# A two-block transformer kernel on one core: some transfers issued by GpSimd, a rotation put ahead of a head's weights, mask additions and first loads moved

## The chip, the cores and the metric

The kernel runs on one core of one Trainium2 chip. The metric is the device time of one execution in microseconds (us), taken as the median of several. "The trace" is the hardware profiler's record of one execution. TensorE is PE in it (PEld its weight loads), VectorE DVE, ScalarE ACT, GpSimd POOL, SyncE SP; a q behind a name is the engine's queue, where DMAs are issued.

## The reference

Two blocks of two layers each work on 256 tokens of width 1024, all in float32.

The first block's layer is a gated feed-forward (width 2816), a mix of pooling over windows of 2 to 16 tokens and causal attention with 8 heads, and a second feed-forward. The second block's layer, which matters here, is cut to its core:

```python
proj = x @ w_in[i]
q_na, k_na, v_na, q_r, k_r, v_r, g_r, gate_a, gate_b = jnp.split(proj, IN_SPLITS, axis=-1)
ya = neighbourhood_attention(q_na, k_na, v_na, na_rpb[i])        # 8 heads of 64
yb = bidirectional_retention(q_r, k_r, v_r, g_r, ...)            # 4 heads; q_r, k_r go through rotary()
merged = sigmoid(gate_a) * (ya @ w_branch_a[i]) + sigmoid(gate_b) * (yb @ w_branch_b[i])
x = layer_norm(ALPHA * x + merged @ w_out[i], ...)
ffn = conv_glu_ffn(x, w_up[i], conv_w[i], conv_b[i], w_down[i])
ple = sigmoid(x @ w_ple_gate[i]) * (p[i] @ w_ple_proj[i])
x = layer_norm(ALPHA * x + ffn + ple, ...)
```

`rotary` takes the halves x1, x2 of a head's 128 features and gives x1 cos - x2 sin and x2 cos + x1 sin. In the neighbourhood attention a query sees the keys of 16 columns around it, with a bias (`na_rpb`) for each offset.

## The kernel before

**Weights.** All weights come as one stream of 336 chunks of 128 partitions x 2048 float32 (1 MB) through three slots. SP loads a chunk as soon as its slot's raw copy is free (L452). ACT writes its upper part (`w_hi`, L614), DVE the rest (`w_lo = raw - w_hi`, L1092), and TensorE makes three products of upper and lower parts for each tile, about 5.7 us for a chunk. A slot's parts may be rewritten when TensorE is done with the chunk (`w_used`), so chunk m is followed in its slot by m + 3. In the code `split_after(here, m)` splits the chunk that follows m.

**Order of work.** Each engine has one program, written out by hand, that runs over the chunks (m = 0 to 41 in the mixing part of a layer of the second block, then 33 chunks of feed-forward as A gate, B up, D down). What an engine does beside a chunk stands in its loop at that m, and is done in that order. Semaphores count events: `mix_evac` the results taken out of PSUM in a layer, `qk_ready` the rotated pairs, `qk_turned` and `v_placed` arrived DMAs (16 each), `prod_ready` the products in a feed-forward.

**Neighbourhood attention, m = 5 to 13.** DVE takes the scores of head m - 5 (`softmax_scores`, L1232 to L1242), ACT their exponentials (L710), DVE scales them (`softmax_weights`, L1249, L1253) and turns the corners of head m - 6 (`turn_corners`, L1272, L1273). TensorE transposes the weights of head m - 6 after chunk m and multiplies two heads with the values (`weigh_near_values`, L2131) after chunks 8, 10, 12 and 14. That needs the corners of both heads and all values in `v_tok`.

**Values and pair halves.** Value rows leave PSUM at m = 5 (`mix_evac` 5 and 6). `place_values` sorts them from row order into `v_tok` by four DMAs for each of two tiles (64 KB each, L746). The retention's q and k are made as pairs n = 0 to 3 of 128 features x 2 x 256 at m = 6 to 9 (`mix_evac` 7 to 10; the first three are sums made by DVE, the last is ACT's evacuation at L964). `turn_halves` (L713) swaps a pair's halves by two DMAs (128 KB each) into one of two places, by n % 2. `turn_pairs` on DVE (L1281, L1282, L1285) multiplies by sine and cosine and adds. Both DMA helpers are issued from ACT's queue here, at m = 5, 6 and 6 to 9, and `turn_pairs(n)` stands at m = n + 7 behind the head's weights and corners, ahead of the split.

**Tables and masks.** `load_tables` on GpSimd (L553) loads `rpb` and `pT` of a layer and adds the window mask to the bias of each head (L561, eight additions). It runs after the pooling for layer 0, and for layer 1 right after the first layer norm of layer 0. GpSimd's `decays` (L579 to L585) come at the head of a layer, and its next work is at the retention.

**First loads.** The first two chunks come in four pieces of 128 x 512 (L437, L439), and the input `xT` in four as well (L782). TensorE runs 22 warm-up matmuls meanwhile (L2140).

## Time and profile before

| | us |
|---|---|
| runs | 1938.16, 1938.36, 1939.33 |
| median | 1938.36 |
| the profiled execution, device time | 1938.22 |
| its span, first to last instruction | 1936.4 |
| TensorE busy in it | 1918.9 (99%) |
| VectorE, ScalarE, GpSimd busy | 1386.9, 1030.9, 167.3 |

The span is what the views below count from: a row of the timeline gives start and duration in us, engine, line, operation, output and inputs, and in brackets the idle time of the engine before it with what ended it. The execution's own time is 1.82 us more than its span. TensorE is the engine that sets the end, so a stretch is read from its gaps.

### The profile page before, as it was taken

To read this page: it belongs to the slowest core of one execution; us is meant where nothing else is said; L and a number is where in the kernel's file an instruction comes from. 1 tells how busy PE (TensorE), PEld (TensorE's weight loads), DVE (VectorE), ACT (ScalarE), POOL (GpSimd) and SP (SyncE) were. 2 spreads that over 40 slices of the span, in tenths; PEclk is the share of its full clock that TensorE was granted. 3 is DMA by queue.
4 is the path that set the end of the run, shared out by engine and by line. 5 is a ranking of instruction groups with operands and counts; after the bars stand their busy time and mean duration, and the time that the engine had idled before them with its cause. 6 is when DMAs were issued, how large, how long until landed. Compare 5 with 4: busy or idle time off the path is not lost.

```text
span 1936.4 us, 26395 instructions
## 1 busy us (share of the span) xinstructions
PE 1918.9 (99%) x9942; PEld 1626.9 (84%) x9942; DVE 1386.9 (72%) x1700; ACT 1030.9 (53%) x1195; POOL 167.3 (9%) x147
## 2 busy tenths in 40 slices
PE   9999999999999999999999999999999999999998
PEld 8888878888888888788888878878888878888887
DVE  7666777666776667768667666577889676677887
ACT  6444665544454455655444554456566554456664
POOL 1000230000000004103002201020001401000000
PEclk9999999999999999999999999999999999999999
DMA  8555545555455545446555554565553654555552
GB/s 335 190 182 185 203 143 185 186 185 192 174 197 194 192 155 209 162 173 228 194 184 186 180 180 152 213 225 182 195 195 138 211 185 160 210 202 192 193 193 111
DMA packets 54362, 365.37 MB, mean 189 GB/s; under 512 B 6416, under 2 KB 7696, under 8 KB 11280
## 3 DMA queue, kind: packets, MB, share of 16 engines
q1 hardware_dynamic: 49392, 349.66, 50.1%
q0 software_dynamic: 1616, 9.96, 1.4%
q10 hardware_dynamic: 3280, 4.72, 0.8%
q8 instruction: 51, 0.84, 0.2%
q14 instruction: 23, 0.19, 0.0%
HBM read 360.12 MB, written 1.05 MB: 187 GB/s over the span
## 4 chain that ended last, share of the span: by engine, by line
PE 92%; DVE 3%; ACT 2%; issue 2%; ACTq 0%; DMA 0%; POOL 0%; POOLq 0%; SPq 0%; DVEq 0%
PE up_two L1865 13%; PE gate_two L1865 13%; PE up_two L1870 7%; PE gate_two L1870 7%; PE gate_two L1796 6%; PE gate_two L1798 5%; PE gate_two L1797 5%; PE low_two L1796 5%; PE low_two L1797 5%; PE low_two L1798 5%; PE bank L1796 5%; PE bank L1798 5%; PE bank L1797 5%; DVE w_lo L1092 1%; PE low_two L1865 1%
## 5 line engine op out<-in xcount | busy, mean ns | idle before, releaser
L1092 DVE TENSOR_TENSOR w_lo<-raw,w_hi 128x2048 fp32r<-128x2048 f32 x315 | 728.7, 2314 | 204.6 <-ACT w_hi L614 198.9
L614 ACT ACTIVATE w_hi<-raw 128x2048 fp32r<-128x2048 f32 x319 | 608.7, 1909 | 102.5 <-PE low_two L1798 32.1
L1865 PE MATMUL up_two<-br_parts,w_hi 128*128 128x512 f32 x1152 | 276.6, 391 | 0.0
L1865 PE MATMUL gate_two<-br_parts,w_hi 128*128 128x512 f32 x1120 | 273.9, 390 | 0.9 <-DVE w_lo L1295 0.7
L1865 PEld LDWEIGHTS gate_two<-br_parts,w_hi 128*128 128x128 f32 x1120 | 209.4, 188 | 45.0 <-issue 1.8
L1865 PEld LDWEIGHTS up_two<-br_parts,w_hi 128*128 128x128 f32 x1152 | 211.9, 188 | 41.4
L1796 PE MATMUL gate_two<-w_lo,br_parts 128*128 128x512 f32 x480 | 192.1, 400 | 1.0 <-ACT area L931 0.9
L1798 PE MATMUL gate_two<-w_hi,br_parts 128*128 128x512 f32 x480 | 187.4, 390 | 0.0
L1797 PE MATMUL gate_two<-w_hi,br_parts 128*128 128x512 f32 x480 | 187.0, 390 | 0.0
L1870 PE MATMUL gate_two<-br_parts,w_lo 128*128 128x256 f32 x1120 | 155.2, 283 | 0.0
L1870 PEld LDWEIGHTS up_two<-br_parts,w_lo 128*128 128x128 f32 x1152 | 148.7, 191 | 5.5
L1870 PE MATMUL up_two<-br_parts,w_lo 128*128 128x256 f32 x1152 | 151.9, 283 | 0.0
L1870 PEld LDWEIGHTS gate_two<-br_parts,w_lo 128*128 128x128 f32 x1120 | 147.2, 191 | 4.9
L669 ACT ACTIVATE hid_hi<-area 128x512 fp32r<-128x512 f32 x58 | 36.7, 632 | 170.5 <-PE bank L1798 107.8
L664 ACT ACTIVATE area<-gate_two 128x512 f32<-128x512 f32 x68 | 40.5, 595 | 136.0 <-PE gate_two L1870 136.0
L664 ACT ACTIVATE area<-up_two 128x512 f32<-128x512 f32 x68 | 40.7, 598 | 130.0 <-PE up_two L1870 129.9
L1796 PEld LDWEIGHTS gate_two<-w_lo,br_parts 128*128 128x128 f32 x480 | 90.1, 188 | 23.1 <-issue 5.7
L1798 PEld LDWEIGHTS gate_two<-w_hi,br_parts 128*128 128x128 f32 x480 | 90.1, 188 | 19.5
L1797 PEld LDWEIGHTS gate_two<-w_hi,br_parts 128*128 128x128 f32 x480 | 90.3, 188 | 17.6
L1149 DVE TENSOR_TENSOR area<-area,up_two 128x512 f32<-128x512 f32 x68 | 46.5, 684 | 62.2 <-ACT area L664 62.2
L1796 PE MATMUL low_two<-w_lo,hid_hi 128*128 128x512 f32 x232 | 91.0, 392 | 0.0
L1797 PE MATMUL low_two<-w_hi,hid_lo 128*128 128x512 f32 x232 | 91.0, 392 | 0.0
(329 smaller groups left out, 2974.4 us busy)
## 6 DMA issues: line engine op xcount, KB each, us to landing
raw<-stream SPq DMA_DIRECT2D x328, 1024.0 KB, 4.8
area<-rows POOLq DMA_DIRECT2D x4, 1024.0 KB, 5.1
area<-rpb POOLq DMA_DIRECT2D x2, 1280.0 KB, 7.6
raw<-stream SPq DMA_DIRECT2D x8, 256.0 KB, 7.5
konst<-consts SPq DMA_DIRECT2D x1, 1600.0 KB, 8.3
area<-rows POOLq DMA_DIRECT2D x2, 768.0 KB, 4.8
area<-xT ACTq DMA_DIRECT2D x4, 256.0 KB, 6.7
x<-x_rows SPq DMA_DIRECT2D x1, 1024.0 KB, 10.9
```

The costliest lines, as they stand in the source:

```text
L614: act.activation(w_hi[:, s, :], raw[:, s, :], ACT.Copy).then_inc(hi_ready[s], 1)
L664: return act.activation(out, pair[:, :, 1, :], ACT.Copy)
L669: act.activation(place[:, 0:2, :], hidden, ACT.Copy).then_inc(hid_hi_ready.sem, 1)
L1092: dve.tensor_tensor(w_lo[:, s, :], raw[:, s, :], w_hi[:, s, :].bitcast(F32), ALU.subtract).then_inc(lo_ready[s], 1)
L1149: return dve.tensor_tensor(out, out, pair[:, :, 0, :], ALU.add)
L1796: pe.matmul(out, whi, xlo, start=start, stop=False, skip_group_check=True)
L1797: pe.matmul(out, wlo, xhi, start=False, stop=False, skip_group_check=True)
L1798: return pe.matmul(out, whi, xhi, start=False, stop=stop, skip_group_check=True)
L1865: pe.matmul(pair[:, f, :, :], w_hi[:, s, at:at + P], parts[:, :, k, :], start=k == 0, stop=False, skip_group_check=True)
L1870: return pe.matmul(pair[:, f, 0, :], w_lo[:, s, at:at + P], parts[:, 0, k, :], start=False, stop=k == DT - 1, skip_group_check=True)
```

## The change

In `place_values` and `turn_halves` the engine becomes GpSimd; they are called in its program between the decays and the retention, values first. `turn_halves` waits for other counts there. `turn_pairs` moves ahead of `softmax_weights` in DVE's loop. `load_tables` waits for a product of a feed-forward: for layer 0 the first of the last one in the first block, for layer 1 the first of layer 0's. The host lays out the first two chunks and `xT` so that each piece is contiguous in HBM, and `stretch` reads them so; what arrives in SBUF is the same.

```diff
@@ -253,6 +253,10 @@
         def piece(j):
             return slice(j * CHUNK // HALVES, (j + 1) * CHUNK // HALVES)
 
+        def stretch(chunk, j):
+
+            return chunk.rearrange("p n -> (p n)").rearrange("(j p n) -> j p n", j=HALVES, p=P)[j]
+
         def by_piece(last, s, pieces):
 
             return [pieces] * (HALVES - 1) + [last[s]]
@@ -434,9 +438,9 @@
 
             sp.dma_start(col1[:, :, :].rearrange("p l c -> p (l c)"), cols1).then_inc(col1_in, 16)
             for j in range(HALVES):
-                sp.dma_start(raw[:, 0, piece(j)], stream[0][:, piece(j)]).then_inc((piece_full[0] + [raw_full[0]])[j], 16)
+                sp.dma_start(raw[:, 0, piece(j)], stretch(stream[0], j)).then_inc((piece_full[0] + [raw_full[0]])[j], 16)
             for j in range(HALVES):
-                sp.dma_start(raw[:, 1, piece(j)], stream[1][:, piece(j)]).then_inc((piece_full[1] + [raw_full[1]])[j], 16)
+                sp.dma_start(raw[:, 1, piece(j)], stretch(stream[1], j)).then_inc((piece_full[1] + [raw_full[1]])[j], 16)
             sp.dma_start(raw[:, 2, :], stream[2]).then_inc(raw_full[2], 16)
             sp.dma_start(konst[:, 0:MATRICES], consts[:, 0:MATRICES]).then_inc(matrices_in, 16)
             for s in range(SLOTS):
@@ -489,6 +493,24 @@
                 for a in range(TT):
                     pool.wait_ge(ln_var.sem, here.at(ln_var, TT * n + a + 1))
                     pool.tensor_tensor(rs[:, a:a + 1], ms[:, a:a + 1], minus_half, ALU.pow).then_inc(ln_rs.sem, 1)
+
+            def place_values(here, tile):
+
+                pool.wait_ge(mix_evac.sem, here.at(mix_evac, 5 + tile))
+                for r in (2 * tile, 2 * tile + 1):
+                    for a in range(TT):
+                        first = r % TT * GRID_W + a * HALF_W
+                        pool.dma_start(v_tok[r:P:GRID_ROWS, a, :], v_by_row[first:first + HALF_W, tile, :]
+                                       ).then_inc(v_placed.sem, 16)
+
+            def turn_halves(here, n):
+
+                two, place = ret_qk[:, 2 * n:2 * n + 2, :], turned_places[n % 2]
+                pool.wait_ge(mix_evac.sem, here.at(mix_evac, n + 7 if n < 2 else 10))
+                if n >= 2:
+                    pool.wait_ge(qk_ready.sem, here.at(qk_ready, n - 1))
+                for at, other in ((0, TURN), (TURN, 0)):
+                    pool.dma_start(place[at:at + TURN], two[other:other + TURN]).then_inc(qk_turned[n % 2].sem, 16)
 
             def load_rows(n):
 
@@ -550,8 +572,9 @@
                                        ).then_inc(pool_d.sem, 1)
                 norm(here, 2)
 
-            def load_tables(l, n):
-
+            def load_tables(l, n, before):
+
+                pool.wait_ge(prod_ready.sem, before)
                 pool.dma_start(area4[:, 0:HEADS * TT * NEAR], rpb[bass.ds(l, 1)].rearrange("a p n -> (a p) n")
                                ).then_inc(bias_in, 16)
                 pool.dma_start(flat(ple_in[:, :, :]), pT[bass.ds(l, 1)].rearrange("a p n -> (a p) n")
@@ -563,7 +586,7 @@
 
 
             pool.wait_ge(pool_y.sem, DEPTH)
-            load_tables(0, 1)
+            load_tables(0, 1, Place(0, DEPTH - 1).at(prod_ready, PAIRS + 1))
             for layer in range(DEPTH):
                 here = Place(1, layer)
                 cur = col2[:, layer, :]
@@ -584,6 +607,12 @@
                 for h in range(RET_HEADS):
                     pool.tensor_tensor(decays[:, h, :], decays[:, h, :], backward[:, h, :], ALU.add
                                        ).then_inc(dist_ready.sem, 1)
+
+                for tile in range(TT):
+                    place_values(here, tile)
+                pool.wait_ge(dist_ready.sem, here.at(dist_ready, RET_HEADS))
+                for n in range(4):
+                    turn_halves(here, n)
 
                 for h in range(RET_HEADS):
                     pool.wait_ge(ret_var.sem, here.at(ret_var, h + 1))
@@ -599,7 +628,7 @@
                 pool.wait_ge(ple_split.sem, here.at(ple_split, 1))
                 layer_norm(here, 0)
                 if layer < DEPTH - 1:
-                    load_tables(layer + 1, layer + 2)
+                    load_tables(layer + 1, layer + 2, here.at(prod_ready, 1))
                 else:
                     pool.wait_ge(base_ready.sem, here.at(base_ready, DT))
                     load_rows(2 * layer + 1)
@@ -711,14 +740,6 @@
                                        accum_out=stat[:, b, 4 + a:5 + a])
                 e.then_inc(exp_ready.sem, 1)
 
-            def turn_halves(here, n, two):
...
             def weights_out(here, h, keys):
 
                 act.wait_ge(p_turned.sem, here.at(p_turned, h + 1))
@@ -737,15 +758,6 @@
                 act.activation(out, banks[6][:, 0, :].rearrange("p (a n) -> p a n", a=TT), ACT.Copy
                                ).then_inc(pT_ready.sem, 1)
 
-            def place_values(here, tile):
...
             def attention_out(here, j):
 
                 act.wait_ge(pv_done.sem, here.at(pv_done, 2 * j + 2))
@@ -779,7 +791,7 @@
                                ).then_inc(by_piece(hi_ready, s, piece_hi[s])[j], 1)
 
             for j in range(HALVES):
-                act.dma_start(flat(x_first[:, 2 * j:2 * j + 2, :]), xT[:, j * 2 * T:(j + 1) * 2 * T]).then_inc(x_in[j], 16)
+                act.dma_start(flat(x_first[:, 2 * j:2 * j + 2, :]), stretch(xT, j)).then_inc(x_in[j], 16)
             act.wait_ge(small_set, SMALL)
             act.activation(ms[:, :], small[:, 0:TT], ACT.Silu)
             act.wait_ge(col1_in, 16)
@@ -941,8 +953,6 @@
                             act.wait_ge(branch_evac.sem, here.at(branch_evac, 2))
                         act.wait_ge(wide_half.sem, here.at(wide_half, wide_ends.index(m) + 1))
                         wide_out(0, m)
-                        if m == 5:
-                            place_values(here, 0)
                     chunk_done(here, m)
                     bank = banks[4 + m % 2]
                     if m in wide_ends:
@@ -978,13 +988,6 @@
                         near_attention_out(here, (m - 8) // 2)
                     if 0 <= m - 5 < HEADS:
                         softmax_exp(here, m - 5, NEAR_KEYS, lambda a: 1.0)
-                    if m == 6:
-                        place_values(here, 1)
-                    if 6 <= m < 10:
-                        if m == 6:
-                            act.wait_ge(dist_ready.sem, here.at(dist_ready, RET_HEADS))
-                        act.wait_ge(mix_evac.sem, here.at(mix_evac, m + 1))
-                        turn_halves(here, m - 6, two)
                     if 0 <= m - 18 < RET_HEADS:
                         h = m - 18
                         act.wait_ge(ret_turned.sem, here.at(ret_turned, h + 1))
@@ -1650,12 +1653,12 @@
                                               ALU.mult).then_inc(ple_mul.sem, 1)
                     if m >= 8 and m % 2 == 0 and (m - 8) // 2 < HALVES:
                         near_attention_lower(here, (m - 8) // 2)
+                    if 7 <= m < 11:
+                        turn_pairs(here, m - 7, ret_qk[:, 2 * (m - 7):2 * (m - 6), :], K_COS2, K_SIN2)
                     if 0 <= m - 5 < HEADS:
                         softmax_weights(here, m - 5, NEAR_KEYS)
                     if 0 <= m - 6 < HEADS:
                         turn_corners(here, m - 6)
-                    if 7 <= m < 11:
-                        turn_pairs(here, m - 7, ret_qk[:, 2 * (m - 7):2 * (m - 6), :], K_COS2, K_SIN2)
                     s = m % SLOTS
                     if m == 33:
                         dve.wait_ge(hi_ready[s], here.uses(m) + 2)
@@ -2464,6 +2467,10 @@
     return part.reshape(-1, P, part.shape[1]).transpose(1, 0, 2).reshape(P, -1)
 
 
+def _stretches(chunk):
+    return chunk.reshape(P, HALVES, -1).transpose(1, 0, 2).reshape(P, -1)
+
+
 def _ffn_chunks(up, down, held=0):
     whole = slice(None)
 
@@ -2519,7 +2526,7 @@
         chunks += _ffn_chunks(a["w_up_2"][l], a["w_down_2"][l], held=1)
     out = np.empty((STREAM, P, CHUNK), np.float32)
     for n, c in enumerate(chunks):
-        out[n] = c
+        out[n] = _stretches(c) if n < 2 else c
     assert len(chunks) == STREAM
     return out
 
@@ -2549,7 +2556,7 @@
     entry = (rows_off + NA_ROWS - 1) * (2 * NA_COLS - 1) + cols_off + NA_COLS - 1
     rpb = a["na_rpb_2"].reshape(DEPTH, HEADS, -1)[:, :, entry].transpose(0, 2, 1, 3, 4).reshape(DEPTH, P, -1)
     arrays = {
-        "xT": _tile(a["x"][0].T, slice(None), slice(None)),
+        "xT": _stretches(_tile(a["x"][0].T, slice(None), slice(None))),
         "x_rows": a["x"][0].reshape(TT, P, D).transpose(1, 0, 2).reshape(P, -1),
         "stream": _stream(a),
         "cols1": cols1,
```

## Rows read from the trace of the kernel before

**Rows 1.** The page's first part, and the cores with span and granted clock.

```profile
PE 1918.9 (99%) x9942; PEld 1626.9 (84%) x9942; DVE 1386.9 (72%) x1700; ACT 1030.9 (53%) x1195; POOL 167.3 (9%) x147
...
core 0: 1936.4 us, clock 0.999
```

**Rows 2.** Start of the kernel: timeline of TensorE, and two windows with DMA share and GB/s.

```profile
1.11 6.98 PE L2140 MATMUL low_two<-softT 128*128 128x256 f32 x22 [1.11 <-POOL small L466]
...
8.40 0.47 PE L1865 MATMUL gate_two<-br_parts,w_hi 128*128 128x512 f32 x1 [0.32 <-DVE w_lo L1295]
...
10.46 0.47 PE L1865 MATMUL gate_two<-br_parts,w_hi 128*128 128x512 f32 x1 [0.43 <-DVE w_lo L1295]
...
2.00:3.00 1.00, 1.00 (x4) 0.73 (x4) 0.00 (x0) 0.35 (x1) 0.00 (x0) 1.00 0.86 197
...
7.00:8.00 1.00, 1.00 (x6) 0.61 (x4) 0.43 (x1) 1.00 (x3) 0.00 (x0) 1.00 1.01 367
```

**Rows 3.** Timeline of TensorE, neighbourhood attention of layer 0: its four gaps.

```profile
1101.96 0.76 PE L2131 MATMUL up_two<-softT,area 128*64 128x160 f32 x8 [0.17 <-issue]
...
1116.35 0.76 PE L2131 MATMUL up_two<-softT,area 128*64 128x160 f32 x8 [0.83 <-issue]
...
1124.67 0.47 PE L1796 MATMUL gate_two<-w_lo,br_parts 128*128 128x512 f32 x1 [0.44 <-ACT area L931]
...
1130.75 0.76 PE L2131 MATMUL up_two<-softT,area 128*64 128x160 f32 x8 [0.36 <-issue]
```

**Rows 4.** Timelines of GpSimd, DVE and TensorE at the first layer norm, layers 0 and 1.

```profile
1275.29 0.57 POOL L555 DMA_DIRECT2D area<-rpb  x1
...
1281.17 9.95 POOL L561 TENSOR_TENSOR area<-area,konst 128x320 f32<-128x320 f32 x8 [4.77 <-DMA area<-rpb]
...
1286.23 4.16 DVE L1107 TENSOR_TENSOR br_parts<-area,br_parts 128x256 fp32r<-128x256 f32 x4
...
1728.01 1.47 DVE L1107 TENSOR_TENSOR br_parts<-area,br_parts 128x256 fp32r<-128x256 f32 x4
...
1286.36 0.50 PE L1808 MATMUL gate_two<-w_lo,br_parts 128*128 128x512 f32 x1 [0.39 <-DVE w_lo L1092]
...
1293.33 0.50 PE L1796 MATMUL low_two<-w_lo,br_parts 128*128 128x512 f32 x1 [1.13 <-DVE w_lo L1092]
```

**Rows 5.** Timelines of ACT (and its queue), DVE and TensorE in the same attention.

```profile
1092.84 1.86 ACTq L720 DMA_DIRECT2D area<-area  x2
1094.75 1.91 ACT L614 ACTIVATE w_hi<-raw 128x2048 fp32r<-128x2048 f32 x1 [3.25 <-issue]
...
1103.29 0.69 DVE L1285 TENSOR_TENSOR area<-area 128x512 f32<-128x512 f32 x1
...
1115.08 0.17 DVE L1249 RECIPROCAL stat<-stat 128x2 f32<-128x2 f32 x1 [1.00 <-ACT soft L710]
...
1108.57 0.28 PE L1798 MATMUL gate_two<-br_parts,w_hi 128*128 128x256 f32 x1
```

**Rows 6.** One line's answer, L720 on ACT's queue; then L523, 256 KB from GpSimd.

```profile
DMA to landing us min/median/max: 3.2/4.5/5.6
...
L523 POOL DMA_DIRECT2D area<-rows x2: 543/547/551, 227.0 to 746.6; - x2
...
DMA to landing us min/median/max: 5.4/5.6/5.7
```

**Rows 7.** DMA issues by line (KB each, median us to landing): pair 2, and the page's tables.

```profile
area<-area ACTq DMA_DIRECT2D x2, 128.0 KB, 4.5
...
area<-rpb POOLq DMA_DIRECT2D x2, 1280.0 KB, 7.6
```

**Rows 8.** Timelines in feed-forwards: DVE and TensorE in layer 0's, GpSimd at 887.

```profile
1337.59 2.29 DVE L1092 TENSOR_TENSOR w_lo<-raw,w_hi 128x2048 fp32r<-128x2048 f32 x1 [1.04 <-ACT w_hi L614]
...
1343.16 0.40 PE L1796 MATMUL low_two<-w_lo,hid_hi 128*128 128x512 f32 x1
...
887.24 13.54 POOL L561 TENSOR_TENSOR area<-area,konst 128x320 f32<-128x320 f32 x8 [8.37 <-DMA area<-rpb]
```

More of the change, by code:

```diff
@@ L712, in softmax_exp @@
                 e.then_inc(exp_ready.sem, 1)
-            def turn_halves(here, n, two):
-                place = turned_places[n % 2]
-                if n >= 2:
-                    act.wait_ge(qk_ready.sem, here.at(qk_ready, n - 1))
-                for at, other in ((0, TURN), (TURN, 0)):
-                    act.dma_start(place[at:at + TURN], two[other:other + TURN]).then_inc(qk_turned[n % 2].sem, 16)
             def weights_out(here, h, keys):
@@ L738, in near_weights_out @@
                                ).then_inc(pT_ready.sem, 1)
-            def place_values(here, tile):
-                act.wait_ge(mix_evac.sem, here.at(mix_evac, 5 + tile))
-                for r in (2 * tile, 2 * tile + 1):
-                    for a in range(TT):
-                        first = r % TT * GRID_W + a * HALF_W
-                        act.dma_start(v_tok[r:P:GRID_ROWS, a, :], v_by_row[first:first + HALF_W, tile, :]
-                                      ).then_inc(v_placed.sem, 16)
             def attention_out(here, j):
```

## The prediction

> **What bounds the kernel now.** I read the profile's page first: TensorE is busy 1918.9 of 1936.4 us and the granted clock is 0.999 [rows 1]. So a change that removes no matmul can win only out of TensorE's 17.5 us without one, and I listed its gaps from the timeline. Those of 0.1 us or more add up to 10.3 us. They are the first 1.11 us, 0.32 and 0.43 us at the first weight pieces [rows 2], four gaps in the neighbourhood attention of each layer of the second block, 0.17 + 0.83 + 0.44 + 0.36 = 1.80 us in its layer 0 and 1.85 us in layer 1 [rows 3], 0.39 + 1.13 = 1.52 us after the first layer norm of layer 0 [rows 4], and 2.4 us at a layer's end that the change doesn't touch. Everything below moves one of these or opens a new one. A measurement of this kernel can tell 0.2%, 3.9 us, from no change.
>
> **Part 1, values and pair halves issued by GpSimd.** Per layer ACT loses 16 DMA issues. Two for a pair's halves take 1.86 us on its queue, and with the four for the values ahead of them they hold the split of chunk 6 back: 3.25 us of idle, until 1094.75 [rows 5]. DVE's low part of that chunk then ends at 1098.9 and DVE trails TensorE by some 4 us for the next five chunks; its period there is 7.2 us (scores at 1106.11 and 1113.31). That lag makes the 0.83 and the 0.36: DVE has the corners of head 3 at 1116.24, after its wait until 1115.08 [rows 5], and TensorE goes on at 1116.35 [rows 3]. With the issues on GpSimd, idle from 1075 until 1160 in this layer, the split starts at 1091.5 and DVE is ahead by 3.2 us minus 0.6 that TensorE's scores cost it, so about 2.6.
>
> GpSimd's queue in order: four value DMAs after the first evacuation (1080.7), four after the second (1083.8), at 0.55 us each [rows 6] done by 1086.1; then pair 0 after its sum (1090.9), pair 1 after 1097.6. These have more than 4 us before DVE wants them. The next one doesn't. Pair 2 used to leave as soon as its sum was made, at 1107.5. Now it waits for count 10 of the evacuations, which ACT's evacuation of chunk 9 gives (count 9 could come from ACT as well as from DVE, and GpSimd, unlike ACT, can't know which). TensorE ends chunk 9 at 1108.7 [rows 5] and ACT needs 0.6 us, so count 10 comes at 1109.35, the two issues are at 1109.4 and 1110.0, and what arrives is the question. Ends for issue to landing: 3.2 us (the fastest of the eight issued by ACT [rows 6]) and 7.6 us (GpSimd's table of 1280 KB [rows 7], far larger). I take 4.6, nearest to the same transfer into the same place, 4.5 from ACT [rows 7]. Arrival: 1114.6.
>
> **Part 2, rotation ahead of the weights.** Per chunk DVE waits 1.00 us for ACT's exponentials (0.41 to 0.67 where a sum fills it) [rows 5], and the rotation (three operations, 1101.89 to 1103.98, 2.1 us) can hide that: 0.4 to 1.0 us of DVE time per chunk, against weights that come 1.1 to 1.7 us later after the scores. By hand for layer 0: at chunk 7 rotation 0 runs 1097.6 to 1099.7, corners done 1100.9, TensorE asks at 1101.8, so the 0.17 goes. At chunk 8 corners are done at 1108.2, in time. At chunk 9 DVE has its scores at 1111.3 but the rotation now stands in front of weights, corners and split, and waits for the arrival at 1114.6; it ends at 1116.7, weights 1117.5, corners 1117.9. TensorE, which asks at 1115.35, goes on at 1118.0: a gap of 2.6 us for 0.83. At chunk 10 DVE has scores 1120.95, lower half 1121.35, rotation 3 (long arrived) 1123.45, weights 1124.15; TensorE asks at 1124.65, no gap. ACT's split no longer stands before its evacuation of chunk 11, so the 0.44 goes: chunk 12 starts at 1125.8 for 1124.67, +1.1. The 0.36 goes too (corners 1129.9, asked 1131.5). **+0.8 us a layer, +1.6 for both.** Each 1 us of landing moves this by 1 us: at 3.2 us it is -0.6, with the old gaps at -1.8 the floor; at 5.6 (slowest of the eight) +1.8; at 7.6 +3.8.
>
> The rows price the issue (0.55 us [rows 6]) but not this transfer from GpSimd; its nearest in size, 256 KB, landed in 5.6 us behind one of 768 KB [rows 6]. The Trainium skill (DMA: Bandwidth & Descriptors, Latency and other measured facts) gives a first byte after about 1 us for a transfer issued by GpSimd and 0.6 for one by ACT; by that the landing would be 0.4 us more, the sum 0.8 more. No row has the same transfer from both.
>
> **Part 3, masks in the next feed-forward.** In layer 0 the eight additions of the window run at 1281.17 for 9.95 us, right in the layer norm. DVE's four subtractions of a tile pass take 4.16 us there and 1.47 in layer 1, which loads no tables [rows 4]. With the other operations in that stretch DVE loses some 4.6 us, and 0.39 + 1.13 us of it reach TensorE; layer 1 has no gap there. The change takes these 1.52 us away. What it puts in their place: the additions start 5.9 to 9.5 us (two observed arrivals) after the first product of the second block's feed-forward, ended 1322.8, so at 1329 to 1332, and end about 1342. There DVE has half a dozen two-operand operations in SBUF between 1328 and 1336, each of which can lose some 0.6 us as those subtractions did: 3.6 to 5.0 us. The product at 1334.3 releases ACT's split of the down chunk and that the low part at 1337.59, done 1339.88; TensorE asks for it at 1343.16, so 3.3 us are covered [rows 8]. A new gap of 0 to 1.7 us, of which I take 0.6; later rounds are idle for 2.7 of 17 us and catch up. For layer 0's tables the additions move only from 887 to some 5 us later within the same kind of feed-forward; they took 13.54 us there and no gap followed [rows 8], so nothing. **-0.9 us**, ends -1.5 and +0.2. The row is explained by the Trainium skill (SBUF — State Buffer, on the shared port pair): a DVE instruction with two SBUF inputs and a GpSimd instruction that reads SBUF exclude one another for a whole instruction. It speaks against the new place as much as the old, since the taps have two SBUF inputs as well.
>
> **Part 4, first loads contiguous.** Eight weight pieces and four input pieces now read 256 KB in a row instead of 2 KB of every 8. In the third microsecond the engines are 0.86 busy and move 197 GB/s, in the eighth 1.01 and 367 [rows 2]; strided pieces ran in both, so the stride alone isn't slow, but cold and spread reads could be. The cap is short: TensorE is on its warm-up until 8.09 and would start at 8.12 for 8.40, and two more tiles take 1.38 us, so tile 2 would go at 9.50 for 10.46: at most 0.96 us. And chunk 2 waits for the gate sum behind DVE's and ACT's chain from the same pieces. Ends 0 and -0.96; I take **-0.4**. The Trainium skill (Perfetto Trace Analysis, Contiguity and DMAs) says contiguity matters only within an SBUF partition line, and that isn't changed; by that this term is 0 and the sum 0.4 more.
>
> **Sum.** +1.6 - 0.9 - 0.4 = +0.3 us. The profiled execution took 1938.22 us, 1.82 around its span and 0.14 below the median; on it 1938.5, on the median 1938.7. I forecast **1938.6 us**, no change.
>
> **Rivals.**
> *Slower: the late pair 2.* The place is DVE at chunk 9 of each layer. The mechanism is in the sum already; it decides when the landing is 6.4 us or more, +2.6 a layer, +5.2 less 1.3 = +3.9. At 7.6 us it gives 7.6 - 1.3 = +6.3, 1944.7 us. For it: one raw chunk of 1 MB starts at the same time, GpSimd's tables took 7.6 us [rows 7], and four transfers now leave back to back. Against: the eight small ones landed in 3.2 to 5.6. The Trainium skill (SBUF — State Buffer, the trap of DVE blocking DMA) adds that DVE in a two-port operation keeps GpSimd from writing descriptors; the table issue at 1275.29 took 0.57 us [rows 4], with DVE in a subtraction from 1275.44 on, which shows no such hold. Chance 0.13.
> *Faster: everything overlaps.* If pair 2 arrives within 3 us or so and the first loads come at full rate: -3.65 - 1.52 - 0.96 = -6.1, 1932.2 us. Beyond -3.9 it needs landings at 3.2 us in both layers, the whole start and no new gap. Against: the wait for count 10, which no landing removes. Chance 0.07.
> *Masks only trade places.* The feed-forward gives back the 1.52 us in full (+1.7): +1.6 + 0.2 - 0.4 = +1.4, 1939.6 us. Still no change; chance 0.15, within the 0.80.
> *The contiguous loads do nothing*, as the packets stay 2 KB on the SBUF side: +0.7, 1938.9 us. Chance 0.4 beside the others.
>
> **How the numbers follow.** No change holds 0.80: forecast 0.65 and the masks' rival 0.15. Range: at the low end landings of 3.2 us (-1.2), masks -1.5 and the start -0.96, -3.7; at the high end 5.6 us (+3.6) and masks +0.2, +3.8. Trimmed a little below, where three ends must meet: 1935.2 to 1942.4.
>
> **What would show it.** Per layer: no idle before ACT's split of chunk 6, the gap before the first and third value product gone, and at the second one a gap of some 2.6 us in place of 0.83, DVE idle 3 us before a rotation with a DMA as releaser. Near 1286 and 1293 no gap, DVE's subtractions 0.4 us each; at 1343 a gap of under 1.7 us. Tile 2 of the first chunk between 9.5 and 10.5. It is wrong if the second value product waits under 0.8 us (landing or order misread), if TensorE stalls in the feed-forward by over 2 us, or if the values arrive after 1101.

## The result, and the profile after

The changed kernel takes **1942.16 us** (median of 14 runs, 1940.58 to 1943.48). The kernel before, run beside it, takes 1938.53 us (14 runs, 1937.77 to 1939.74). The ratio is 1.0019, 95% interval 1.0011 to 1.0026: 3.6 us slower, just short of the 0.2% (3.9 us) up to which the prediction counts a difference as none. The profiled execution took 1942.77 us, 1.77 more than its span.

The page's first part, and the cores, as in [rows 1]:

```profile
PE 1921.3 (99%) x9942; PEld 1631.7 (84%) x9942; DVE 1383.7 (71%) x1700; ACT 1030.7 (53%) x1195; POOL 186.7 (10%) x179
...
core 0: 1941.0 us, clock 0.997
```

The span grew by 4.6 us, about 1 us more than the medians differ: the profiled execution lies 0.6 us above its median, that of the kernel before 0.3 below. TensorE has the same 9942 matmuls, but is busy 2.4 us longer, and the granted clock went from 0.999 to 0.997: part of the loss is inside its work. So I set the two timelines of TensorE side by side, matmul by matmul (all 9942 stand in both in the same order), and noted where the later kernel's lead or lag changes. That ledger is my own working from the two traces:

```
stretch                                  lag at its end   change   forecast
start, to the third chunk (20)               -1.17         -1.17     -0.4
attention of layer 0 (1101 to 1140)          +1.65         +2.82     +0.8
layer norm and feed-forward (1286 to 1345)    0.00         -1.65     -0.9
attention of layer 1 (1545 to 1586)          +4.61         +4.61     +0.8
end                                          +4.61         +4.61     +0.3
```

**Attention.** TensorE's timeline, where [rows 3] had 0.17, 0.83, 0.44 and 0.36 in layer 0. One gap is left there, and one in layer 1:

```profile
1117.94 0.77 PE L2134 MATMUL up_two<-softT,area 128*64 128x160 f32 x8 [3.87 <-issue]
1118.64 0.49 PE L2120 MATMUL up_two<-konst,soft 128*128 128x128 f32 x2
1118.83 0.72 PE L1799 MATMUL gate_two<-w_lo,br_parts 128*128 128x512 f32 x1
1119.35 0.63 PE L1800 MATMUL gate_two<-w_hi,br_parts 128*128 128x512 f32 x1
...
1563.26 1.34 PE L2134 MATMUL up_two<-softT,area 128*64 128x160 f32 x8 [4.43 <-issue]
```

It is the second value product, as predicted. Behind it a matmul of 512 columns takes 0.63 us and not 0.39. The windows of TensorE's work (length, busy time of PE, PEld, DVE, ACT and POOL, then the granted clock, DMA share and GB/s) tell why:

```profile
1114.00:1118.00 4.00, 0.13 (x3) 0.09 (x3) 3.11 (x9) 0.00 (x0) 0.00 (x0) 1.00 0.24 70
1118.00:1120.00 2.00, 2.00 (x13) 1.58 (x14) 2.00 (x1) 0.66 (x2) 0.00 (x0) 0.72 0.00 0
1120.00:1122.00 2.00, 2.00 (x6) 1.52 (x6) 1.97 (x10) 1.10 (x5) 0.00 (x0) 0.50 0.27 33
1122.00:1126.00 4.00, 4.00 (x19) 3.22 (x18) 3.78 (x8) 2.11 (x2) 0.00 (x0) 0.96 0.59 246
1559.00:1563.00 4.00, 0.00 (x0) 0.00 (x0) 2.82 (x8) 0.00 (x0) 0.00 (x0) 0.95 0.25 65
1563.00:1565.00 2.00, 1.74 (x11) 1.33 (x11) 1.97 (x2) 0.00 (x0) 0.00 (x0) 0.50 0.00 0
1565.00:1567.00 2.00, 2.00 (x7) 1.61 (x6) 1.97 (x9) 1.44 (x6) 0.00 (x0) 0.50 0.30 33
```

TensorE did nothing for 3.87 and 4.43 us, and then ran some 3 and 6 us at 0.50, its 1.2 GHz level, before it was back at 2.4 GHz. By the ledger that cost 1.57 us in layer 0 and 2.75 us in layer 1, on top of 3.05 and 3.58 us by which the gaps outgrew the 0.83 and 0.85 of before. The other three gaps went, and with the short steps around them gave back 1.80 us in layer 0 and 1.72 in layer 1.

DVE, GpSimd and SyncE's queue at that place:

```profile
1106.63 2.29 DVE L1095 TENSOR_TENSOR w_lo<-raw,w_hi 128x2048 fp32r<-128x2048 f32 x1
...
1109.46 0.17 DVE L1243 TENSOR_SCALAR stat<-stat 128x2 f32<-128x2 f32 x1
1114.67 0.69 DVE L1284 TENSOR_TENSOR area<-area,konst 128x512 f32<-128x512 f32 x1 [5.05 <-DMA area<-area]
...
1108.37 1.18 POOL L513 DMA_DIRECT2D area<-area  x2 [10.51 <-ACT area L974]
...
1109.10 0.33 SPq L456 DMA_DIRECT2D raw<-stream  x1
```

DVE had its scores at 1109.6 and stood until 1114.67 for pair 2, which GpSimd issued at 1108.37 and 1108.95, when ACT's evacuation of chunk 9 gave the tenth count. L513's own answer for this stretch (it takes in pair 3 too) says how long the four transfers took:

```profile
DMA to landing us min/median/max: 2.3/5.8/6.1
```

The first half landed in 2.3 us, the second in 5.7, pair 3's in 6.0 and 6.1. In layer 1, with the same order of issues, the second half took 6.25 us, and the gap is longer by as much: 4.43 us for 3.87. While GpSimd was issuing the second half (1108.95 to 1109.54), SyncE sent a weight chunk of 1 MB, at 1109.10, since DVE had freed its slot with the low part that ended at 1108.92. The DMA queues in 1110.5 to 1112.4 list one row:

```profile
q1 hardware_dynamic: 57, 0.47, 70.9%
```

q1 carries the weights. q0, GpSimd's, has 48 packets in the 1.0 us before that window, 128 KB in all and so the first half, then 128 packets in the 2.6 us after it, and none within. The second half of pair 2 moved nothing for 1.9 us. The Trainium skill (DMA: Bandwidth & Descriptors, Queues, rings and completion order) says an engine takes turns between its queues packet by packet. By that a small transfer would lose little beside a large one, if its packets stand ready; whether they did in these 1.9 us, the trace doesn't show, so it doesn't test the rule.

**Masks.** At 1286 and 1293 no gap is left where [rows 4] had 0.39 and 1.13, and DVE's four subtractions take 1.47 us for 4.16. In the feed-forward, where [rows 8] had none:

```profile
1328.52 10.31 POOL L584 TENSOR_TENSOR area<-area,konst 128x320 f32<-128x320 f32 x8 [4.85 <-DMA area<-rpb]
...
1327.45 0.87 DVE L1685 SCALAR_TENSOR_TENSOR area<-area,col 128x255 f32<-128x255 f32 x2
...
1332.67 2.11 DVE L1685 SCALAR_TENSOR_TENSOR area<-area,col 128x255 f32<-128x255 f32 x2
...
1340.67 2.29 DVE L1095 TENSOR_TENSOR w_lo<-raw,w_hi 128x2048 fp32r<-128x2048 f32 x1 [1.04 <-ACT w_hi L643]
...
1343.01 0.50 PE L1799 MATMUL low_two<-w_lo,hid_hi 128*128 128x512 f32 x1 [0.25 <-DVE w_lo L1095]
```

The same two taps, DVE's multiply-adds of the feed-forward's convolution, take 0.87 us just ahead of the additions and 2.11 beside them, the low part comes 3.1 us later than in [rows 8], and TensorE waits 0.25 us. With the steps behind that wait the ledger has 0.56 us.

**Start.** TensorE's first real product begins at 8.25 for 8.40, the gap at 10.46 is gone, and the third chunk starts at 20.34 for 21.46. In the third microsecond the DMA engines move 291 GB/s for 197 at the same busy share (0.86):

```profile
2.00:3.00 1.00, 1.00 (x4) 0.72 (x4) 0.00 (x0) 0.35 (x1) 0.00 (x0) 1.00 0.86 291
```

One thing in this stretch is not the loads'. TensorE's warm-up matmuls take 0.63 us each at first and 0.38 later, as the clock rises from its lower level to the upper one, and the time of this rise differs between executions: 5.12 us into the span before, 6.15 in this trace, 3.99 to 6.96 in the twelve profiled kernels. (The clock column of the windows reads 1.00 ahead of it as well; the rise is read from the matmuls' length.) So the warm-up ends at another time in each.

### The profile page after: what moved, and what is told of

Same layout as the page of the kernel before. It is cut to its first block, busy times and chain, and to the rows that moved or that the text cites. A ratio compares the mean times of both kernels' runs of the same rounds, so it can differ in the third digit from the quotient of the medians.

```text
span 1941.0 us, 26396 instructions
## 1 busy us (share of the span) xinstructions
PE 1921.3 (99%) x9942; PEld 1631.7 (84%) x9942; DVE 1383.7 (71%) x1700; ACT 1030.7 (53%) x1195; POOL 186.7 (10%) x179
## 3 DMA queue, kind: packets, MB, share of 16 engines
q10 hardware_dynamic: 720, 1.57, 0.2%
## 4 chain that ended last, share of the span: by engine, by line
PE 95%; DVE 2%; issue 1%; ACT 1%; POOL 0%; POOLq 0%; ACTq 0%; DVEq 0%
PE up_two L1868 13%; PE gate_two L1868 13%; PE up_two L1873 7%; PE gate_two L1873 7%; PE gate_two L1799 6%; PE gate_two L1801 6%; PE gate_two L1800 6%; PE low_two L1799 5%; PE low_two L1800 5%; PE low_two L1801 5%; PE bank L1799 5%; PE bank L1801 5%; PE bank L1800 5%; PE low_two L1868 1%; PE low_two L2396 1%
```

## What the experiments had to tell apart

The question is how much of the loss is the wait for pair 2, and what made it. Theory: pair 2 leaves late (it waits for a count that comes 5 us after its sum) and lands late, and the rotation, now ahead of the weights, turns that into a gap of TensorE, which also costs its clock. Rivals: the late departure alone does it; the moved rotation costs by itself; GpSimd's issues are slow; the clock's fall is only a sign of the gap. Each run below is timed beside the kernel before, whose median was 1938.4 to 1939.0 us.

| run | what it is | us | ratio to before, 95% |
|---|---|---|---|
| e1 | changed kernel, pair 2 leaves with its own sum | 1930.24 | 0.9955 (0.9941 to 0.9968) |
| e2 | changed kernel, rotation behind the weights | 1930.35 | 0.9956 (0.9942 to 0.9970) |
| e3 | changed kernel, ACT issues the halves | 1930.46 | 0.9957 (0.9943 to 0.9970) |
| e9 | changed kernel, one weight chunk behind pair 2 | 1930.49 | 0.9960 (0.9947 to 0.9974) |
| e4 | changed kernel, the wait filled with products | 1939.18 | 1.0001 (0.9992 to 1.0010) |
| e7 | before, with GpSimd's issues alone | 1933.09 | 0.9972 (0.9961 to 0.9982) |
| e8 | before, with the moved rotation alone | 1936.87 | 0.9991 (0.9982 to 1.0000) |
| e5 | before, with the moved masks alone | 1937.16 | 0.9991 (0.9982 to 1.0000) |
| e6 | before, with the contiguous loads alone | 1936.95 | 0.9994 (0.9985 to 1.0003) |
| e10 | e1, masks four pairs later | 1930.80 | 0.9963 (0.9949 to 0.9976) |

## Three ways out of the wait

**e1.** Pair 2 waits for its own sum. That may be the ninth count from DVE or ACT, so a second wait makes sure that DVE's is in.

```diff
-                pool.wait_ge(mix_evac.sem, here.at(mix_evac, n + 7 if n < 2 else 10))
+                pool.wait_ge(mix_evac.sem, here.at(mix_evac, n + 7))
+                if n == 2:
+                    pool.wait_ge(att_ready.sem, here.at(att_ready, 1))
```

> The changed kernel with one wait altered: pair 2's transfers leave when its own sum is made, one chunk earlier. If the late pair 2 and the lower TensorE clock behind its gap are the cause (theory), both gaps of 3.9 and 4.4 us go, the granted clock stays 1.00 through the attention, the four old gaps stay away too, and the time is 1932 to 1933 us, some 10 us under the changed kernel. If GpSimd as the issuing engine is the cause (rival 1: its transfers are slow whenever they leave), a gap of over 1 us stays and the time is above 1938. If the rotation ahead of the weights costs by itself (rival 2), DVE still waits over 1 us for a DMA at a rotation.

Measured 1930.24 us, 1.8 below the range I expected. GpSimd and DVE:

```profile
1103.35 1.19 POOL L515 DMA_DIRECT2D area<-area  x2 [6.24 <-DVE att_lo L1112]
...
1108.72 0.17 DVE L1245 TENSOR_SCALAR stat<-stat 128x2 f32<-128x2 f32 x1
1108.80 0.68 DVE L1286 TENSOR_TENSOR area<-area,konst 128x512 f32<-128x512 f32 x1
```

The pair leaves 5 us earlier and DVE rotates it straight after the scores. No gap of over 0.15 us is left in the attention. Against before each attention loses 2.7 us by the ledger, not the 1.8 that its four gaps add up to in [rows 3]: 0.24 at the first value product, 0.89, 0.25, 0.51, 0.43 and 0.32. The short steps between those gaps had been missed by a list of gaps.

The clock stayed up in both attentions, but fell at another place, at the end of layer 0, where it didn't fall in e2. First e1's windows, then e2's (the columns are those of the windows above):

```profile
1482.00:1486.00 4.00, 2.04 (x18) 1.64 (x16) 3.31 (x10) 1.83 (x4) 0.95 (x1) 1.00 0.00 0
1486.00:1490.00 4.00, 4.00 (x21) 4.00 (x22) 3.06 (x9) 3.96 (x11) 0.00 (x0) 0.57 0.01 4
...
1483.00:1487.00 4.00, 2.04 (x18) 1.64 (x16) 3.33 (x9) 1.83 (x4) 0.95 (x1) 1.00 0.00 0
1487.00:1491.00 4.00, 3.85 (x29) 3.66 (x30) 3.06 (x9) 3.96 (x11) 0.00 (x0) 1.00 0.02 4
```

TensorE's gaps ahead of it are 0.43, 1.23 and 0.74 us, and every profiled execution has them. Only e1's and e5's show a fall behind them, of 3.41 us, and lose 1.0 and 0.9 us there by the ledger. It is probably a part of how much executions of one kernel differ: of the 24 of the kernel before beside e5, the eight that took longest, 1938.83 us and more, are those with a granted clock of 0.998, and the others, at 0.999, took 1938.69 or less. So a difference of under 1 us between medians is taken for none below.

**e2.** The rotation goes back behind weights, corners and value product; the pair still leaves late.

```diff
-                    if 7 <= m < 11:
-                        turn_pairs(here, m - 7, ret_qk[:, 2 * (m - 7):2 * (m - 6), :], K_COS2, K_SIN2)
...
                     if 0 <= m - 6 < HEADS:
                         turn_corners(here, m - 6)
+                    if 7 <= m < 11:
+                        turn_pairs(here, m - 7, ret_qk[:, 2 * (m - 7):2 * (m - 6), :], K_COS2, K_SIN2)
```

> The changed kernel with the rotation back behind a head's weights and corners. Theory: pair 2 still arrives late and DVE waits 3 to 4 us for it, but with weights and corners of the head already out, so only the split and the next head's weights are late: a gap of about 1 us at the second value product or the chunk after it, no fall of the clock, 1934 to 1935 us. Rival 1 (GpSimd's transfers are slow as such): values or pairs late everywhere, above 1938. Rival 2 (order alone): 1933, as e1.

Measured 1930.35 us. I had expected the late pair to cost some gap even here, and it costs none. DVE and SyncE's queue:

```profile
1107.44 2.28 DVE L1095 TENSOR_TENSOR w_lo<-raw,w_hi 128x2048 fp32r<-128x2048 f32 x1
...
1112.63 0.69 DVE L1284 TENSOR_TENSOR area<-area,konst 128x512 f32<-128x512 f32 x1
...
1109.90 7.53 SPq L456 DMA_DIRECT2D raw<-stream  x2
...
DMA to landing us min/median/max: 2.2/2.3/4.2
```

DVE comes to the rotation at 1112.63, 3.0 us later than it asked for it in the changed kernel (1109.63), and waits for nothing there. But the transfers landed sooner as well. Pair 2 left at 1108.48 as in the changed kernel (1108.37), and yet both of its halves landed in 2.3 us (the 4.2 is the first half of pair 3). With the rotation behind, DVE's low part ends at 1109.72 and not 1108.92, so SyncE sends the 1 MB chunk at 1109.90, after both halves are on the queue. This gave a new theory: the moved rotation itself made pair 2's transfer late, by freeing a slot 0.8 us sooner. It also means that e2 doesn't show what a late landing costs a rotation that stands behind the weights: there was none.

**e9** tests it. The weight chunk at that place (chunk 194, and 269 in layer 1) waits on SyncE until pair 2 has landed; everything else is the changed kernel.

```diff
+            def refill(n, held=None):
+                for s in range(SLOTS):
+                    sp.wait_ge(lo_ready[s], n)
+                    if held is not None and s == 2:
+                        here = Place(1, held)
+                        sp.wait_ge(qk_turned[0].sem, here.at(qk_turned[0], 2 * 16 * P // TURN))
...
+            first = 2
+            for held, at in enumerate((64, 89)):
+                with sp.Fori(first, at) as n:
+                    refill(n)
+                refill(at, held)
+                first = at + 1
```

> The changed kernel with one wait more on SyncE, once in each layer: the weight chunk that it issued at 1109.10, 0.6 us before GpSimd's second transfer of pair 2 moved its first packet, is held until both transfers of pair 2 have landed. Theory: the second half is late because the 1 MB chunk is ahead of it, so both halves now land in some 2.3 us, VectorE goes on near 1111.4 instead of 1114.67, the gap at the second value product is 0.3 to 1.0 us instead of 3.87, the clock stays at 1.00, and the time is 1931.0 to 1932.5. Rival: the landing of some 5.6 us is the transfer's own (GpSimd's descriptors, the small packets), whatever else is on the queues: the wait and the gap stay and the time is 1941.5 to 1943.

Measured 1930.49 us, 0.5 below the expected range: one wait more takes 11.7 us off the changed kernel. GpSimd issues at 1107.45, DVE and SyncE go on so:

```profile
1110.32 0.69 DVE L1296 TENSOR_TENSOR area<-area,konst 128x512 f32<-128x512 f32 x1 [1.62 <-DMA area<-area]
...
1110.37 0.33 SPq L460 DMA_DIRECT2D raw<-stream  x1
...
1113.60 0.76 PE L2146 MATMUL up_two<-softT,area 128*64 128x160 f32 x8 [0.45 <-issue]
...
area<-area POOLq DMA_DIRECT2D x2, 128.0 KB, 2.2
```

The halves land in 2.2 and 2.3 us (2.3 and 5.7 in the changed kernel), the wait falls from 5.05 to 1.62 us, the gap from 3.87 to 0.45, and the clock stays at 1.00. So the chunk beside the second half is what made it late. (The expectation lets the second half's packets begin 0.6 us behind the chunk's issue; by the count of q0's packets above those were still the first half's.) The other kernels' rows, whichever engine issues the pair (the chunk's issue is SyncE's row nearest to the pair's, ahead or behind):

```
pair 2 in                 halves issued    1 MB chunk issued   landing, us
before (ACT)              1107.5, 1108.2   1106.36             4.5, 4.6
e3 (ACT)                  1103.9, 1104.6   1102.76             4.6, 4.6
e1 (GpSimd)               1103.4, 1103.9   1101.34             3.7, 4.0
changed kernel (GpSimd)   1108.4, 1108.9   1109.10             2.3, 5.7
e4 (GpSimd)               1107.7, 1108.2   1108.38             2.3, 6.2
e2 (GpSimd)               1108.5, 1109.1   1109.90             2.2, 2.3
e9 (GpSimd)               1107.4, 1108.0   1110.37             2.2, 2.3
```

How much a chunk costs is not fixed by this order alone. In e1 the next chunk is issued at 1108.36, 0.21 us behind the second half of pair 3, and that half lands in 3.7 us; in the changed kernel 0.14 us made 5.7. And in e2, from 1112 to 1115 us, pair 3 and the chunk move side by side, 57 packets of q0 and 106 of q1. By which mechanism the chunk holds a small transfer back, in the engines or in what feeds them, no run here tells.

**e3.** ACT issues the pairs' halves, as before; rotation, masks, loads and GpSimd's issue of the values stay changed.

```diff
-                for n in range(4):
-                    turn_halves(here, n)
...
+                    if 6 <= m < 10:
+                        if m == 6:
+                            act.wait_ge(dist_ready.sem, here.at(dist_ready, RET_HEADS))
+                        act.wait_ge(mix_evac.sem, here.at(mix_evac, m + 1))
+                        turn_halves(here, m - 6, two)
```

> The changed kernel with the pair halves issued from ACT's queue again, as before the change (pair 2 after its own sum); values from GpSimd, rotation ahead, masks and loads as changed. Theory: like e1, 1932 to 1933.5 us, no gap over 0.3 us in the attention. Rival 1 (the engine): also fast, so it must be told apart by e1. Rival 2 (rotation ahead costs as such): above 1936.

Measured 1930.46 us, again below the range, with no gap of 0.1 us in the attentions. The issues cost ACT nothing that reaches TensorE once the values' eight are gone from its queue.

## What the clock's fall costs

**e4.** Sixteen products on the identity, whose results nobody reads, go ahead of the second value product.

```diff
+                    if m == 10:
+                        fill_wait(16)
                     if m >= 8 and m % 2 == 0 and (m - 8) // 2 < HALVES:
                         weigh_near_values(here, (m - 8) // 2)
```

> The changed kernel with 16 calls of a dummy product (3.7 us by the row of the same call at the layer's end) in TensorE's wait before the second value product. The wait itself stays. Theory: with the clock's fall as a part of its own, the granted clock stays 1.00 behind the wait and the time falls by the 1.6 + 2.7 us that matmuls at half clock cost in the two layers, to 1937.5 to 1938.5 us. If the fall had another reason than the idle stretch, the time is that of the changed kernel, 1942, or more.

Measured 1939.18 us (1937.80 to 1940.34), 3.0 us below the changed kernel and 0.7 above the expected range. In its profiled execution the clock column reads 1.00 in both attentions, and its timeline and the changed kernel's, laid side by side, part by 1.58 us behind the gap of layer 0 and by 2.84 us behind that of layer 1, 4.4 us together, with the value product itself at about the same time (1117.76 for 1117.94). The trace lists each of the sixteen as two:

```profile
1113.20 3.73 PE L2148 MATMUL low_two<-konst 128*128 128x128 f32 x32
1117.76 0.76 PE L2134 MATMUL up_two<-softT,area 128*64 128x160 f32 x8 [0.83 <-issue]
...
1118.96 0.39 PE L1800 MATMUL gate_two<-w_hi,br_parts 128*128 128x512 f32 x1
```

So the fall is a cost of its own, not a sign of the gap: 4.4 us in these two executions, 3.0 by the medians. The profiled execution of e4 is the shortest of its 11, and what the others lost was not traced. The remaining 9 us to e1 are the wait and what it holds up.

## The parts alone

**e7.** The kernel before, with `place_values` and `turn_halves` moved to GpSimd as in the change, all else undone.

> The kernel before with one part of the change: GpSimd issues the pair halves and the values; rotation, masks and first loads are as before. Theory: ScalarE's split of chunk 6 is no longer held 3.25 us, VectorE is not late after it, the four gaps of each attention go (2.7 us with what follows each of them, twice), pair 2's later transfer lands before the rotation that stands behind the weights asks for it, and the time is 1933.0 to 1934.2. Rival: the gaps are VectorE's own load in that stretch and only go when the rotation is moved: 1938 to 1939.

Measured 1933.09 us, as expected; every gap of both attentions is gone. It is worth 5.35 us, the largest single part. Pair 2 leaves late here too (1109.76) and lands in 2.2 and 2.3 us, as SyncE's chunk comes behind both halves, at 1111.16. So a late departure with the rotation behind costs nothing.

**e8.** The kernel before, with `turn_pairs` ahead of `softmax_weights` and nothing else.

> The kernel before with one part of the change: the rotation ahead of the head's weights, ScalarE still issues everything. Theory: the four gaps come from ScalarE's hold of chunk 6's split by the issues of the values, which stays, so VectorE is still late, and at the second value product the head's weights now come behind the 2.0 us of rotation and not behind 1.0 us of waiting for the exponential: that gap grows from 0.83 to some 1.8 us in each layer, the time is 1939.5 to 1941.5. Rival: the rotation in that idle time is what cures the lateness, as with the halves on ScalarE and the rest of the change: 1933 to 1934.5.

Measured 1936.87 us, between the two; by time alone that could be no change, since the interval reaches 1. The gap I expected is there, but at the first value product:

```profile
1100.77 0.68 DVE L1281 TENSOR_TENSOR area<-area,konst 128x512 f32<-128x512 f32 x1
...
1103.72 0.20 DVE L1273 STREAM_TRANSPOSE softT<-soft 32x32 f32<-32x32 f32 x1
...
1104.03 0.76 PE L2131 MATMUL up_two<-softT,area 128*64 128x160 f32 x8 [1.75 <-issue]
```

DVE is still late from ACT's hold of chunk 6 and puts 2.1 us of rotation ahead of the corners: 1.75 us for 0.17. After that the rotation fills the waits for the exponentials, DVE catches up within two chunks, and the other gaps go, 2.4 us in each layer. So the rotation ahead is worth 0.9 and 1.0 us in the two layers with ACT's issues, by the ledger. With GpSimd's it is worth nothing when pair 2 is in time (e1 and e2 differ by 0.1 us), and costs 11.8 us where it lets the chunk in ahead of pair 2.

**e5.** The kernel before, with the wait for the next feed-forward in `load_tables` alone:

```diff
+                pool.wait_ge(prod_ready.sem, before)
```

> The kernel before with one part of the change: the masks' additions wait for the next feed-forward. Theory: the two steps at the first layer norm of layer 1 go (0.4 to 0.6 and 1.3 us), VectorE's late residual in the feed-forward costs 0.4 back, and the time is 1.3 to 1.8 us under the kernel before, 1937.0 to 1937.8. Rival: the additions cost in their new place what they cost in the old: 1938.5 to 1939.5.

Measured 1937.16 us, 1.3 us down, and the interval reaches 1 here too. The ledger shows the steps of the changed kernel: -2.22 us at the layer norm (-0.55 and -1.29 in two of them) and +0.53 in the feed-forward. This profiled execution has the fall of the clock at the layer's end, which took 0.9 us back.

**e6.** The kernel before, with the contiguous first loads alone:

```diff
-                sp.dma_start(raw[:, 0, piece(j)], stream[0][:, piece(j)]).then_inc((piece_full[0] + [raw_full[0]])[j], 16)
+                sp.dma_start(raw[:, 0, piece(j)], stretch(stream[0], j)).then_inc((piece_full[0] + [raw_full[0]])[j], 16)
```

> The kernel before with one part of the change: the first weight chunks and xT come as contiguous stretches. Theory: the split of the first chunks starts earlier, the gap of 0.43 us at 10.46 goes, and the start is shorter by 0.8 to 2.0 us: 1936.5 to 1937.8. Rival: the first loads take what they took, since each piece still comes in the same number of bytes per partition: 1938.2 to 1938.8.

Measured 1936.95 us, 1.5 us down, which the timing alone (its interval takes in 1) would leave open. TensorE's lead at the third chunk is 1.4 us and stays so to the end, and the third and fourth microseconds move more (the fourth of the kernel before comes first here, its third is in [rows 2]):

```profile
3.00:4.00 1.00, 1.00 (x4) 0.82 (x3) 0.00 (x0) 0.99 (x2) 0.00 (x0) 1.00 0.88 223
...
2.00:3.00 1.00, 1.00 (x4) 0.72 (x4) 0.00 (x0) 0.34 (x1) 0.00 (x0) 1.00 0.94 272
3.00:4.00 1.00, 1.00 (x4) 0.81 (x3) 0.00 (x0) 0.99 (x2) 0.00 (x0) 1.00 1.04 393
```

In the fourth microsecond the eight profiled kernels with these loads move 363 to 414 GB/s, the four without them 223 to 266. In the other seven with these loads the lead over the kernel before is 0.8 to 2.1 us; in e5, e7 and e8, which have its loads, the start differs from its own by -0.2 to +0.5. In all of the eight but e10 the lead follows the rise of the clock in the warm-up: 0.8 us in e3, where it rose at 6.96 us, 2.0 in e9, where it rose at 4.40. The sooner the warm-up ends, the more the earlier data are worth.

**e10.** In e1 the masks wait for the fifth hidden product of the feed-forward:

```diff
-                    load_tables(layer + 1, layer + 2, here.at(prod_ready, 1))
+                    load_tables(layer + 1, layer + 2, here.at(prod_ready, 5))
```

> The kernel of the first run (pair 2 leaves with its own sum), and the masks' additions wait for the fifth hidden product of the feed-forward and not for the first. Theory: every pair of the feed-forward has the same work on VectorE, so the additions slow its taps there as they did at 1328, and TensorE again waits some 0.25 us, one pair of chunks later than they run: 1930.0 to 1930.6. Rival: the first pair has less slack than a later one, no gap, and the time is 0.4 us lower, 1929.6 to 1930.0.

Measured 1930.80 us, no better. The gap at 1343 is gone, as the rival had it, but a new one stands at the end of the feed-forward, which neither foresaw:

```profile
1473.35 0.47 PE L1801 MATMUL low_two<-w_lo,att_hi 128*128 128x512 f32 x1 [0.80 <-DVE att_lo L1112]
```

DVE is late there from the additions:

```profile
1383.87 11.74 POOL L586 TENSOR_TENSOR area<-area,konst 128x320 f32<-128x320 f32 x8 [4.92 <-DMA area<-rpb]
...
1472.52 0.69 DVE L1112 TENSOR_TENSOR att_lo<-area,att_hi 128x512 fp32r<-128x512 f32 x1
```

Beside them single taps of DVE take 1.10 us for 0.48 in e1. DVE, 1.6 us ahead of e1 before them, is 2.4 us behind after them, and at 1472.52 still 1.4.

**The sum.** Alone, GpSimd's issues, masks and loads give 5.35 + 1.28 + 1.46 = 8.1 us. Together, in e2, they give 8.6. They add up, within what medians of such runs can tell. What turned 8.6 us of gain into 3.6 of loss is the fourth part, the rotation ahead, by way of pair 2's landing: with the chunk held back (e9) or the pair sent sooner (e1) it costs nothing.

## Why the prediction was right, and where it was not

No change at 0.80 and a range to 1942.4 held 1942.16, but barely, and with luck: the forecast 1938.6 was 3.6 us low, and its terms erred by more than that, in both directions.

**The late pair 2: mechanism right, size wrong.** The place, the releaser and the product are those of the prediction, and so is the departure: 1108.37 with TensorE 1.17 us ahead is 1109.5, forecast 1109.4. The failed step is "I take 4.6, nearest to the same transfer into the same place". It measured 5.7 for the second half in layer 0 and 6.25 in layer 1. The prediction had the cause in hand, as evidence for its slower rival ("one raw chunk of 1 MB starts at the same time"), and treated it as a chance, although its own timeline could have dated it: the moved rotation lets DVE's low part end earlier, that frees the slot, and SyncE issues at once. In the transfer whose 4.5 it took, the chunk had been issued 1.15 us ahead. So the gap grew by 3.05 and 3.58 us for the 1.8 of the forecast. The other gaps went as forecast, but with the short steps that I hadn't listed they gave back 1.80 and 1.72 us for the 0.97. The two attentions without the clock came to +1.25 and +1.86 us for +0.8 each.

**The clock: not in the sum at all.** The prediction priced a gap at its own length. Behind 3.87 and 4.43 us of idle TensorE ran at 0.50, and that cost 4.3 us in all. Without it the ledger would have ended at +0.3, the number of the forecast, by errors that cancel. Whether the forecast's gap of 2.6 us would have cost clock stays open: there was no fall behind 1.75 us in e8, and one behind 1.23 and 0.74 in e1 and e5, where most executions have none.

**Masks: -0.9 forecast, -1.65 measured.** The new place cost 0.56 us by the ledger, 0.25 of it the gap, and 0.6 had been forecast. The old place was the mis-sized one: the lag fell by 2.22 us there (1.84 of it in two steps), and not by the 1.52 of the two gaps. The reading of the row stands: the taps beside the additions took 2.11 us for 0.87, as the rule from the Trainium skill (SBUF — State Buffer, on the shared port pair) that was cited for it would have it.

**Start: -0.4 forecast, -1.17 measured, and -1.4 in e6.** The cap of 0.96 was the failed step. It took the end of the warm-up, 8.09, as given, and that moves with the rise of the clock: TensorE's first product came at 7.38 us in e9. And it stopped at the second tile, while the third chunk, named in the same paragraph as a chain of its own, brought 0.4 us more. The rule cited there (the Trainium skill, Perfetto Trace Analysis, Contiguity and DMAs) would have given 0; the eight traces with the contiguous loads speak against it here, with 363 to 414 GB/s in the fourth microsecond for 223 to 266.

**ACT's hold: right.** The 3.25 us is gone, the 0.17, 0.44 and 0.36 with it. e7 puts it at 5.35 us for both layers, where the prediction had -3.65 as the floor, since the short steps between the gaps go too. **GpSimd kept from its descriptors by DVE**, the rule weighed under the slower rival: DVE stood idle from 1109.63 to 1114.67 while the second half moved nothing, and in e9 the halves landed in 2.2 us behind the same operations of DVE. So nothing here points to such a hold.

**The faster rival** stopped at -6.1 us, the sum of the listed gaps; e2 reached -8.6. By the prediction's own terms its conditions (landings of 3.2 us, the whole start, no new gap) give only -3.7. And the gaps of 0.1 us or more add up to 9.7 us in the trace before, not 10.3; nothing hung on that.

## What to carry to other kernels

When a change lets an engine finish something sooner, ask which buffer that frees, which large transfer it starts, and which small urgent one then comes behind it; a landing time read from a trace holds only with the same neighbours on the queues. Send a small transfer when its own data is ready and not at the next convenient count (e1, 11.9 us), or hold the large one until it has landed (e9, 11.7). Putting the rotation back behind the others' work (e2, 11.8) helped in the same way, as the large one then left later; what that order is worth with a late landing was not run. And price a gap of several microseconds on TensorE at more than its length: here two of 3.9 and 4.4 us cost 1.6 and 2.8 us more in the work behind them.

## What was not expected of the hardware

- A transfer of 128 KB issued by GpSimd landed in 2.2 to 2.3 us with no large one beside it, and in 5.7 to 6.3 (changed kernel and e4, both layers) with a chunk of 1 MB issued 0.14 us behind it; for 1.9 us none of its queue's packets moved. With the chunk 0.21 us behind it (e1, pair 3) it landed in 3.5 to 3.7.
- After 3.87 us of idle TensorE was at 1.2 GHz for some 3 us, after 4.43 us for some 6 us: the same cause cost 1.6 and 2.8 us in one execution. Sixteen products in the wait kept it at 2.4 GHz.
- The same gaps at a layer's end, 1.23 us the longest, were followed by a fall in two of twelve profiled executions and by none in ten. Its rise at the start came between 3.99 and 6.96 us.
- A list of gaps of TensorE understated what a late DVE cost: 1.8 us of gaps in the attention before, 2.7 us by the ledger when they went.
